# Expert gates applied at the store, and returned rows added by accumulating DMAs instead of VectorE

## The reference

```
logits = xn @ w_router + b_router
top_vals, top_idx = top_k(logits, 2);  weights = softmax(top_vals)
gates[token, e] = weight of e if e is one of the token's two experts, else 0
out = 0
for e in range(8):
    out = out + gates[..., e:e+1] * swiglu(xn, w_gate[e], w_up[e], w_down[e])   # 1024 -> 1792 -> 1024
h = h + out
return rms_norm(h, final_norm)
```

## Time and profile before

| what | value |
|---|---|
| median of three runs | 1008.78 us |
| the profiled execution: its own time, and its span | 1007.8 us, 1006.0 us |
| TensorE busy (matmul) | 982.1 us, 98% of the span |
| VectorE, ScalarE, POOL busy | 756.4, 656.1, 60.6 us |
| the chain that ended last, by engine | PE 82%, DVE 8%, ACT 3%, DMA 3%, issue 2%, POOL 1% |
| DMA | 287.12 MB, mean 285 GB/s |
| DMA, in the 40th parts 22 to 39 (the experts) | 371 to 407 GB/s, 90% busy or more |
| down weights | 64 issues of 896.0 KB, 9.4 us to landing |
| output rows stored, input rows loaded (SP) | 8 issues each of 512.0 KB, 7.9 and 10.2 us to landing |
| mean granted TensorE clock | 0.997 |

### The profile page before, as it was taken

How to read it: one execution, slowest core, us unless ns; L and a number is a source line. 1 busy time by engine, 2 the same in 40 slices (tenths; PEclk the granted TensorE clock), 3 DMA queues, 4 the chain that set the end, 5 groups by cost and what they waited for, 6 DMA issues and landing times.

```text
span 1006.0 us, 14574 instructions
## 1 busy us (share of the span) xinstructions
PE 982.1 (98%) x4892; PEld 829.4 (82%) x4892; DVE 756.4 (75%) x915; ACT 656.1 (65%) x886; POOL 60.6 (6%) x86
## 2 busy tenths in 40 slices
PE   8999999999999999999999999999999999999995
PEld 6987887888887998988877888888888888888883
DVE  5557665456556566666687989898998989899888
ACT  5555345452445545554596787978879787887964
POOL 1301000000000100000160000000000000000141
PEclk9999999999999999999999999999999999999998
DMA  9843689995566657233669999999999999999992
GB/s 322 237 156 128 189 250 309 289 319 156 200 202 216 220 149 190 103 124 106 219 226 400 399 384 407 378 402 371 390 374 385 406 371 401 373 387 391 381 405 101
DMA packets 150536, 287.12 MB, mean 285 GB/s; under 512 B 12769, under 2 KB 58865, under 8 KB 150498
## 3 DMA queue, kind: packets, MB, share of 16 engines
q1 hardware_dynamic: 147890, 277.64, 77.9%
q0 software_dynamic: 2608, 8.98, 2.6%
HBM read 269.81 MB, written 16.78 MB: 285 GB/s over the span
## 4 chain that ended last, share of the span: by engine, by line
PE 82%; DVE 8%; ACT 3%; DMA 3%; issue 2%; POOL 1%; SPq 1%; DVEq 0%; POOLq 0%; ACTq 0%
PE A L584 20%; PE A L586 20%; PE A L585 20%; PE S L584 4%; PE S L586 4%; PE S L585 4%; DVE lo L1606 3%; PE T L629 2%; DMA raw<-in_moe_w_down 1%; DMA raw<-in_moe_w_up 1%; PE T L1091 1%; ACT hi L1156 1%; PE T L664 1%; PE T L1049 1%; ACT R L1211 1%
## 5 line engine op out<-in xcount | busy, mean ns | idle before, releaser
L1606 DVE TENSOR_TENSOR lo<-raw,hi 128x1024 fp32r<-128x1024 f32 (+4 forms) x532 | 570.8, 1130 | 122.0 <-ACT hi L1156 120.0
L1156 ACT ACTIVATE hi<-raw 128x1024 fp32r<-128x1024 f32 (+4 forms) x532 | 485.2, 981 | 149.6 <-PE A L586 123.3
L584 PE MATMUL A<-lo,xT_hi 128*128 128x512 f32 x820 | 324.1, 395 | 2.5 <-DVE lo L1606 2.4
L586 PE MATMUL A<-hi,xT_hi 128*128 128x512 f32 x820 | 319.9, 390 | 0.0
L585 PE MATMUL A<-hi,xT_lo 128*128 128x512 f32 x820 | 319.6, 390 | 0.0
L584 PEld LDWEIGHTS A<-lo,xT_hi 128*128 128x128 f32 x820 | 154.3, 188 | 35.0 <-DVE lo L1606 3.2
L586 PEld LDWEIGHTS A<-hi,xT_hi 128*128 128x128 f32 x820 | 154.0, 188 | 32.3
L585 PEld LDWEIGHTS A<-hi,xT_lo 128*128 128x128 f32 x820 | 154.3, 188 | 30.2
L584 PE MATMUL S<-lo,xT_hi 128*128 128x512 f32 x224 | 89.1, 398 | 1.0 <-DVE lo L1606 1.0
L586 PE MATMUL S<-hi,xT_hi 128*128 128x512 f32 x224 | 87.5, 391 | 0.0
L585 PE MATMUL S<-hi,xT_lo 128*128 128x512 f32 x224 | 87.4, 390 | 0.0
(11 more groups left out here) (239 smaller groups left out, 884.8 us busy)
## 6 DMA issues: line engine op xcount, KB each, us to landing
raw<-in_moe_w_down SPq DMA_DIRECT2D x64, 896.0 KB, 9.4
raw<-in_moe_w_gate SPq DMA_DIRECT2D x32, 768.0 KB, 8.0
raw<-in_moe_w_up SPq DMA_DIRECT2D x24, 768.0 KB, 7.3
raw<-in_moe_w_gate SPq DMA_DIRECT2D x16, 1024.0 KB, 6.9
raw<-in_moe_w_up SPq DMA_DIRECT2D x32, 512.0 KB, 6.8
raw<-in_moe_w_up SPq DMA_DIRECT2D x16, 1024.0 KB, 8.0
raw<-in_ff_w_gate SPq DMA_DIRECT2D x10, 1024.0 KB, 6.0
raw<-in_ff_w_up SPq DMA_DIRECT2D x10, 1024.0 KB, 7.2
```

The lines of the kernel that those rows point to most:

```text
L584: nc.tensor.matmul(out, stat[0], mov[1], start=start, stop=False)
L586: return nc.tensor.matmul(out, stat[0], mov[0], start=False, stop=stop)
L1156: return nc.scalar.activation(out, in_, ACT.Copy)
L1606: nc.vector.tensor_tensor(piece(lo, SPLIT, u, i), piece(raw, RAW, u, i), piece(hi, SPLIT, u, i).bitcast(F32), ALU.subtract).then_inc(lo_do ...
```

## The change

The gates are scattered (POOL, four indirect DMAs of one element per token) to a DRAM table `gate_slots` that is indexed as the rows of `slots`. In each turn SP loads the 128 gates of the next block into `slot_gate`, one per partition, and `output_rows` multiplies with it on the way to `yrow`. The gathered rows come back already scaled. POOL adds them to `h` with four direct DMAs with `accum_op=ALU.add`: first both tiles of k = 0, then, when these have landed, both of k = 1. VectorE's four `add_rows` go. Its `add_output` waits for all four additions, and its order is changed from (0,0), (0,1), (1,0), (1,1) as (t, c) to (0,0), (1,0), (0,1), (1,1); ScalarE's square sums follow the same order, and POOL's inverse rms of tile 0 waits for three sums, of tile 1 for four. Two small transfers are added where the first block of `slots` is cleared.

```
+    gate_slots = nc.dram_tensor("gate_slots", (BLOCKS * P, 1), F32, kind="Internal").ap()
+    gate_blocks = gate_slots.rearrange("(b p) o -> b p o", p=P)
...
+        slot_gate = sb("slot_gate", [P, 1])
...
                     sp.wait_ge(zero_set, 1)
+                    if b == 0:
+                        zeros = sel[:, :].bitcast(F32)
+                        sp.dma_start(gate_slots.rearrange("(p b) o -> p (b o)", p=P), zeros[:, 0:BLOCKS]
+                                     ).then_inc(zero_in, 16)
+                        sp.dma_start(slot_gate[:, :], zeros[:, 0:1]).then_inc(slot_gate_in, 16)
...
                         sp.dma_start(xrow, slots[bass.ds(ve + 2, 1)].rearrange("b p d -> p (b d)")
                                      ).then_inc(xrow_in, 16)
+                        sp.wait_ge(gates_in, 16 * 2 * NT)
+                        sp.dma_start(slot_gate[:, :], gate_blocks[bass.ds(ve + 1, 1)].rearrange("b p o -> p (b o)"),
+                                     allow_slow_non_contiguous=True).then_inc(slot_gate_in, 16)
...
-                act_copy(yrow[:, c * 512:(c + 1) * 512], S[(S_MOE + c) % 2][:, :]
-                         ).then_inc(s_free[(S_MOE + c) % 2], 1)
+                if c == 0:
+                    act.wait_ge(slot_gate_in, ve * 16 + 16)
+                nc.scalar.activation(yrow[:, c * 512:(c + 1) * 512], S[(S_MOE + c) % 2][:, :], ACT.Copy,
+                                     scale=slot_gate[:, 0:1]).then_inc(s_free[(S_MOE + c) % 2], 1)
...
             for n in range(4):
-                t, c = divmod(n, 2)
+                c, t = divmod(n, 2)
...
-            dve.wait_ge(gates_set, 1)
-            dve.wait_ge(y_back, 16 * 2 * NT)
-            for k in range(2):
-                add_rows(k, 0)
             output_lo(0)
-            add_rows(0, 1)
+            dve.wait_ge(added_in, 16 * 2 * NT)
+            add_output(0, 0)
             output_lo(1)
-            add_output(0, 0)
+            add_output(1, 0)
             add_output(0, 1)
-            add_rows(1, 1)
-            add_output(1, 0)
             add_output(1, 1)
...
+            pool.wait_ge(gates_set, 1)
+            for k in range(2):
+                for t in range(NT):
+                    pool.indirect_dma_start(gate_slots, bass.IndirectOffsetOnAxis(row_to[:, k, t:t + 1], 0),
+                                            gate_row[:, k, t:t + 1], None).then_inc(gates_in, 16)
...
+            pool.wait_ge(y_back, 16 * 2 * NT)
+            for k in range(2):
+                if k:
+                    pool.wait_ge(added_in, 16 * NT)
+                for t in range(NT):
+                    pool.dma_start(h[:, t, :], y_from[k][t], accum_op=ALU.add).then_inc(added_in, 16)
             n = N_FINAL
             for t in range(NT):
-                pool.wait_ge(tile_summed, 2 * t + 2)
+                pool.wait_ge(tile_summed, t + 3)
```

More of the change, by code:

```diff
@@ L389, in build @@
         gate_set, rows_added, tile_summed = sem("gate_set"), sem("rows_added"), sem("tile_summed")
-        gates_set = sem("gates_set")
+        gates_set, gates_in = sem("gates_set"), sem("gates_in")
+        slot_gate_in, added_in = sem("slot_gate_in"), sem("added_in")
         last_gained, last_out = sem("last_gained"), sem("last_out")
@@ L2105, in output_lo @@
                                         ALU.subtract).then_inc(y_lo, 1)
-            def add_rows(k, t):
-                step(nc.vector.scalar_tensor_tensor(h[:, t, :], y_from[k][t], gate_row[:, k, t:t + 1],
-                                                    h[:, t, :], ALU.mult, ALU.add))
             def add_output(t, c):
@@ L2315, in _ @@
             nc.gpsimd.tensor_scalar(rowf[:, 1], rowf[:, 0], r1[:, 8, 1:2], None, ALU.is_lt).then_inc(row_to_set, 1)
-            pool.wait_ge(zero_in, 16 * (BLOCKS - 1))
+            pool.wait_ge(zero_in, 16 * BLOCKS)
             pool.wait_ge(y_stored, 16)
```

## The result

| | median us | lowest to highest | runs |
|---|---|---|---|
| before | 1008.32 | 1007.81 to 1008.89 | 4 |
| after | 1019.95 | 1018.18 to 1023.13 | 4 |

The changed kernel is slower: ratio 1.0119, 95% interval 1.009 to 1.0147, that is 11.6 us between the medians, where 3.4 were forecast. The profiled execution is the fastest of the four: it took 1018.18 us, and its span is 1016.4 us, 10.4 longer than before. The four executions have mean granted clocks of 0.993, 0.993, 0.990 and 0.989 in order of time. So the slower two also had more of the lower clock.

The account below looks back on a forecast made before the run. TensorE was taken to bound the kernel, with the DMA engines full too. Two-pass additions delaying TensorE by 4.45 us, less 1.0 us at the end, gave +3.4 us: 1012.2 us, range 1007.8 to 1018.

Parts of the forecast that it names:

- the gates' scatter in turn 1: Turn 1: four scatters issued by 536 to 543, landing before SP's load at 548.06; 0, at most 2 us.
- R4: Rival: a wait in turn 1 or the late gate load, +1 to +2 us on top of any case; no chance given.
- Two passes: Last turn: each addition costs the DMA engines two passes, 2.1 MB a pair; sum +3.4 to +4.2 us, chance 0.45.
- D: Last turn: delay of the last weight landing by the additions; 2.5 us for one pass, 3.8 to 4.9 for two.
- R1: Rival: an addition moves as a copy does, in one pass; +1.0 us, 1009.8 us, chance 0.27.
- D to TensorE, D - 0.45: Last turn: TensorE's last product ends at 992.4 + D against 992.85; +3.35 to +4.45 us for two passes.
- The second pair: End: the k = 1 additions, issued 1.5 us after the first pair lands, move 4.9 us, land at 996.5 to 999.0.
- half-time case: Two passes, the pair taking the engines half the time: weights 4.9 us later, second pair in time, sum +3.4 us.
- 37% case: Two passes, additions getting 37% of the engines: weights 3.8 us later, second pair 1.9 us late, sum +4.2 us.
- R2: Rival: additions so slow that the second pair becomes the end; +8 us at three passes, +14.5 at four, chance 0.15.
- The end, 1.0 us shorter: End without VectorE's four add_rows: 1.0 us gained if VectorE's pair holds POOL's first tile 1 instruction, 1.9 if free.
- R3: Rival, faster: the first pair doesn't meet the weights, D near 0; 1006.9 to 1007.8 us, chance 0.13.

Follow-up runs that it names:

- a1: Changed kernel with gate table, its loads and scaled copy, but no adding DMAs; VectorE adds the rows in the old order: 1015.63 us against 1008.36.
- c1: As a1, but the gate table's elements lie 64 bytes apart instead of 4: 1008.25 us against 1008.49.
- a2: As a1, without the four gate scatters and the wait for them: 1008.78 us against 1008.36.
- b1: Kernel before plus only the adding DMAs and the new order of the end, no gate table: 1013.70 us against 1008.36.
- d1: The whole change, with the gate table's elements 64 bytes apart: 1013.51 us against 1008.24.
- c3: As b1, but the four adding DMAs are plain copies onto h: 1009.59 us against 1008.49.
- c4: As b1, with the additions held until the first piece of the last weight unit is split: 1015.91 us against 1008.49.
- c2: As a1, packed table, but four plain POOL stores in place of the gate scatters: 1016.06 us against 1008.49.
- a3: As a1, but the gate table's elements lie 512 bytes apart: 1008.45 us against 1008.36.
- d2: Kernel before, with POOL multiplying and adding both gathered rows of tile 1; no table, no adding DMAs: 1010.18 us against 1008.24.

## Why the prediction was wrong

The sign was right. 11.6 us were measured, 3.4 forecast, and 1019.95 lies above the range that ends at 1018.

**The step that failed is the gates' scatter in turn 1**, which the prediction took at "nothing, and 2 us as the upper end". It costs 7.3 us (a1), all of it gone when the elements lie 64 bytes apart (c1) or are not written (a2). The working of that step counted POOL's issues and the landing against SP's next load, and there it held: the gate load was issued in time. What it left out was what the four scatters do to the transfers beside them: the sum has no term for the DMA time of their 512 elements, though the same prediction had called the DMA engines full in the turns. While they are under way, the DMA engines move as little as 110 to 195 GB/s in a window of 4 us (after and a1), where the kernel before has 353 to 416. TensorE runs out of weights, and then works at the lower clock for a time. R4 had the place, "a wait in turn 1", but the wrong mechanism and a price of 1 to 2 us. The sign that the prediction named, a new stall before 957, came, and its reading of it ("it is the gate load") was wrong: the stall was over before the gate load was issued at 552.01.

- *TensorE bound, DMA full, turns 2 to 7 unchanged:* right, 60.00 of 60 us.
- *The scaled copy, the load of 128 gates, the clearing:* nothing, right (a2: -0.05%, and its interval reaches from -0.17 to +0.07%). Whether the last turn's small load costs some tenths of a us can't be told.
- *Two passes:* right. D was set at 3.8 to 4.9 us and measured 4.84, 4.95 in b1 and 4.99 in d1; 197 GB/s alone against 383 for a copy. R1 is out, and its own sum was right too: c3 does what R1 says, +1.1 us (+0.1 to +2.0) against +1.0. The Trainium skill, "Collectives: The Full Stack", section "The bandwidth ceiling: the fold count and why AG ≠ RS ≠ AR", explains the half rate of a collective's add by two source reads on one ring; the 197 and 383 GB/s agree with a half, and the ring itself no run here shows.
- *D to TensorE, D - 0.45:* 4.56 after, where 4.4 follow from D. In b1 it is 1.5 us more and in d1 2.0, by the lower clock behind the stall. The prediction had no term for the clock, neither here nor in turn 1.
- *The second pair:* forecast to land between 996.5 and 999.0; less the 6.71 us it landed at 998.5. That it lies within is in part luck. The terms that the prediction names (first pair at 989 to 991.6, issue 1.5 us, 4.9 us of moving) add up to 995.4 to 998.0, about 1 us less than what it states. After, the first pair landed at 991.1, and from there to the second landing it took 7.4 us, not 6.4. VectorE waited 1.13 us for the second pair. At the distances of the earlier trace rows the first product behind `output_lo` would have let it start at about 1005.0, so the pair itself cost some 0.25 us (estimate). The half-time case had no such wait, the 37% case 1.9 us. R2 is out for the changed kernel.
- *The end, 1.0 us shorter:* 0.88 after and 1.06 in b1. POOL's two instructions for tile 1, beside VectorE's pair, took 1.85 us (1010.62 to 1012.47): more than the 1.2 of the free pair before (0.52 and 0.58), less than the some 2.1 of the case that the prediction took. The last product came 0.5 us behind the end of VectorE's pair.
- *R3, the additions don't meet the weights:* c4 made this true by a wait, and it is +7.4 us. The prediction had it as the fast case because it put in one-pass additions. R3's own delay of 6 us wasn't run; with the 14.7 us of c4, a start at 984.5 would end at 999.2, 5.5 us behind 993.73 (estimate), so it would be slower too.

Without the scatters the sum, +3.4 to +4.2, stands against +5.3 in b1 and d1: 1 to 2 us short, and their profiles put 1.4 and 2.0 us on the clock. The changed kernel's own profile, in which the clock doesn't fall in the last turn, has 4.56 - 0.88 = +3.7 us for the additions, within the sum.

What stays open: why neighbours of 4 bytes hold up the other transfers. The runs show that it depends on the distance, that plain stores do it as well, and that other transfers' packets become slow while it lasts. They don't show where in the path from the DMA engines to DRAM it happens, nor where between 4 and 64 bytes it ends, nor whether it is the distance that counts or that each element starts at its own multiple of 64 bytes. What makes the clock fall behind one stall and not behind another stays open as well.

## What to carry to other kernels

A few small writes can cost more than megabytes: 2 KB of gates cost 7.3 us here, 2 MB of additions 5.3 us. Beside a full weight stream, give scattered elements in DRAM 64 bytes each, as c1 did. An adding DMA took engine time here as for twice its bytes, so it is free only where the engines are idle and nothing waits for two of them in series. A stall can cost more than its own length, since the clock may fall behind it. Work taken off an engine is worth what the engine's place on the last chain gives (here 1 us of 5 us of VectorE's time), and the engine or queue that takes it over is to be priced by what it does to its neighbours, not by its own length.

## What the runs showed that I had not expected

- 2 KB of gates, 512 elements of 4 bytes side by side, cut the traffic of all 16 DMA engines to 54 and 55 GB/s for 8 us (c2, share 1.33 and 0.80), where the kernel before has 353 to 416 GB/s in the windows from 534 to 550. The Trainium skill ("DMA: Bandwidth & Descriptors", "Specifications") says that a transfer below 512 bytes makes the DMA engine read, modify and write. No trace here shows that mechanism. The elements of c1 and a3 are below 512 bytes too and cost nothing, so the size alone isn't what costs here.
- SP's issue of an up-projection load has a median of 0.38 us, and in the kernel before none takes more than 2.32. While this lasted one took 6.06 us after, 6.98 in a1 and 9.98 in c2, but none more than 2.65 in a2 and c1. So a long issue on SP's queue went with slow transfers.
- Behind its waits for weights TensorE's clock fell to the lower of its two levels, or was there when it came back: 0.60 of the full one on average from 542 to 546 after (wait of 4.1 us), 0.50 from 995 to 997 in b1 (2.7 us) and in d1 (1.6 us). A wait of 2.04 us in the last turn after was followed by no such fall (clock 1.00).
- POOL's multiplication of 128 x 1024 took 2.86 us at 978.4 and 4.49 us at 984.1 in d2, both times beside VectorE's splits.
